# The preparation of a delta rule, carried along by the last tiles of an input projection

## The chip, the cores and the metric

The kernel runs on one core of a Trainium2 chip. The metric is the device time of one execution in microseconds. Each core has TensorE (PE in the profile; PEld is its weight loads), VectorE (DVE), ScalarE (ACT), GpSimd (POOL) and SyncE (SP, which here only issues transfers).

## The reference

One layer of a decoder, for 1024 prompt positions and 8 x 8 sample positions, so 1088 token columns in all. The normalised input is multiplied by w_in (1024 x 6400), whose first 1408 columns belong to branch A, the rest to branches B, C and three gates. Branch A, after a token shift, is RWKV-7 time mixing with six heads of 64:

```
w_log = -softplus(-(w0 + tanh(lw) @ w2)) - 0.5;  decay = exp(-exp(w_log))
a = sigmoid(a0 + la @ a2);  g = sigmoid(lg) @ g2
kk = k * k_k / max(sqrt(sum((k * k_k)^2)), 1e-12)        # per head
k = k * (1 + (a - 1) * k_a)
S = S * w_t + (S @ -kk_t) x (kk_t * a_t) + v_t x k_t;  out_t = S @ r_t
o = (groupnorm(out) * ln_w + ln_b + sum(r * k * r_k) * v) * g    # the bonus is the sum times v
```

Branches B and C are attentions; then the branches are merged by their gates, and an FFN follows.

## The kernel before

Everything is fp32 with tokens along the free dimension (T = 1088 columns) and features on the 128 partitions. `build` runs the stages in order, each a block of five instruction streams that wait for each other by semaphores, with a barrier between blocks: `stage_load` (loads and transposes x and the small weights), `a_project`, `a_prepare`, `a_delta_rule`, `a_finish`, then branch B, branch C, the merge and the FFN.

`a_project` goes over 50 tiles t of 128 columns of w_in. For each, SP loads 512 KB of weights into the one buffer `wt`, VectorE casts the high part into `wh` (L124), GpSimd subtracts for the low part `wl` (L129), and TensorE makes 3 chunks x 8 k-tiles x 3 products (L135 to L137) into PSUM banks 0 to 2 or 3 to 5 in turn. VectorE then scales the result into `raw` (L489). In VectorE's loop `weights(t + 1)` stands ahead of the eviction of tile t. Tiles 0 to 10 are branch A's: VectorE mixes in the token shift (L472 to L477) and keeps them in `pa`. Tiles 11 to 49 are stored to DRAM by ScalarE's queue (L455); from tile 26 on (the gates) ScalarE applies a sigmoid first (L453).

`a_prepare` makes from `pa` what the delta rule needs, for three pairs of heads (128 partitions each): two LoRA products (L543) and their sigmoids (L580); the squares of the keys, their sums per head (L548: nine matmuls of two columns), square root and reciprocal, spread again over the partitions (L565); a scan of the log decay (L634) and its exponentials (L596 to L598); the bonus (L559, L617); and the multiplications that leave r, k, a and kk scaled (L663 to L667). It holds `ld`, `cu`, `kk` for all three pairs and uses PSUM banks 0 to 6. The delta rule then works on `pa`, `g.av` and `g.at`; `a_finish` normalises its result, adds the bonus `g.bn` (L1285) and gates it.

Of the kernel before, what the change touches and what calls it, by code (L numbers as in the profile page):

```python
# [157 lines left out]
def build(nc, a, outs, scratch):  # L158

    with ExitStack() as ctx:  # L160
# [40 lines left out]
def stage_load(g):  # L201
# [8 lines left out]
    with ExitStack() as ctx:  # L210
# [3 lines left out]
        crow = sb("crow", [2 * NB, 2 * FF])  # L214
# [168 lines left out]
def stage_branch_a(g):  # L383

    nc = g.nc
    with ExitStack() as ctx:
        sb = lambda name, shape, dt=F32: ctx.enter_context(nc.sbuf_tensor(name, shape, dt))
        g.av = sb("av", [P, PAIRS, T])
        g.at = sb("at", [P, PAIRS, T])
        g.bn = sb("bn", [P, PAIRS, T])  # L390
        g.sc = sb("sc", [P, NU - 1, PAIRS])
        g.scs = sb("scs", [P, PAIRS, NB])
        a_prepare(g)
        a_delta_rule(g)
        a_finish(g)


def a_project(g):
# [3 lines left out]
    nc, a = g.nc, g.a  # L402
    w = a["w_in"][0].rearrange("(k p) f -> p k f", p=P)
    with ExitStack() as ctx:
# [4 lines left out]
        dif = sb("ap_dif", [P, 2, T])  # L409
        names = ("w", "wh", "ws", "mm", "ev", "z", "d", "mix", "sg")  # L410
# [4 lines left out]
        stores = lambda t: len(range(AT + (t - AT) % 2, t + 1, 2))  # L415
        with nc.Block() as block:
            @block.sync
            def _(eng):
# [4 lines left out]
                for i, sem in enumerate(g.s_xs):  # L423
                    eng.wait_ge(sem, 16 * len(range(i, SEQ // P + 1, len(g.s_xs))))
                eng.wait_ge(g.s_ls, 32)
                for t in (IN_TILES - 2, IN_TILES - 1):
                    eng.wait_ge(s_st[t % 2], 16 * stores(t))

# [7 lines left out]
            def _(eng):  # L436
                for t in range(IN_TILES):
# [18 lines left out]

            @block.vector
            def _(eng):
                nc.vector.memset(raw[:, :, 0:1], 0.0).then_inc(s["z"], 1)
                eng.wait_ge(s["z"], 1)  # L460

                def weights(t):
                    if t < IN_TILES:
                        eng.wait_ge(s["w"], 16 * (t + 1))
                        if t >= 2:
                            eng.wait_ge(s["mm"], t - 1)
                        high(eng, wh[:, t % 2], wt[:, :, :]).then_inc(s["wh"], 1)

                def mixed(t):
                    b = t % 2  # L470
                    eng.wait_ge(s["ev"], t + 1)
                    nc.vector.tensor_tensor(dif[:, b, :], raw[:, b, 0:T], raw[:, b, 1:1 + T], ALU.subtract).then_inc(s["d"], 1)  # L472
                    eng.wait_ge(s["d"], 2 * t + 1)
                    nc.vector.tensor_tensor(dif[:, b, SEQ:T:NQ], raw[:, b, 1 + T:1 + TP],
                                            raw[:, b, 1 + SEQ:1 + T:NQ], ALU.subtract).then_inc(s["d"], 1)
                    eng.wait_ge(s["d"], 2 * t + 2)
                    nc.vector.scalar_tensor_tensor(out=g.pa[:, t, :], in0=dif[:, b, :], scalar=g.col("rwkv_mu", t),  # L477
                                                   in1=raw[:, b, 1:1 + T], op0=ALU.mult, op1=ALU.add).then_inc(s["mix"], 1)

                weights(0)  # L480
                for t in range(IN_TILES):
                    weights(t + 1)
                    eng.wait_ge(s["mm"], t + 1)
                    if t >= 2:
                        eng.wait_ge(s["mix"], min(t - 1, AT))
                    if t >= AT + 2:
                        eng.wait_ge(s_st[t % 2], 16 * stores(t - 2))
                    for c, (c0, n) in enumerate(chunks(t)):
                        ins = nc.vector.tensor_tensor(raw[:, t % 2, 1 + c0:1 + c0 + n], g.ps[:, 3 * (t % 2) + c, 0:n],  # L489
                                                      g.inv[:, c0:c0 + n], ALU.mult)  # L490
                    ins.then_inc(s["ev"], 1)
                    if t < AT:
                        mixed(t)


def a_prepare(g):

    nc, a, pa, V_ = g.nc, g.a, g.pa, g.nc.vector  # L500
    R, K, V, LWA = 0, 3, 6, 9
    NJ = SEQ // P + 1
    rows = lambda j: P if j < NJ - 1 else TS
    RATE = -float(np.exp(-0.5))
    with ExitStack() as ctx:
        sb = lambda name, shape, dt=F32: ctx.enter_context(nc.sbuf_tensor(name, shape, dt))
        wa2 = sb("wa2", [P, AW])
        keep = sb("keep", [P, T])
        ld = sb("ld", [P, PAIRS, T])
        cu = sb("cu", [P, PAIRS, T])  # L510
        kk = sb("kk", [P, PAIRS, T])
        tmp = sb("tmp", [P, 2, T])
        ex = sb("ex", [P, 3, T])
        mid = sb("mid", [P, NU - 1, PAIRS])
        end = sb("end", [P, NU - 1, PAIRS])
        ends = sb("ends", [P, PAIRS, NB])
        omk = sb("omk", [P, PAIRS])
        nrm = sb("nrm", [P, PAIRS, NJ, 2])
        names = ("w", "th", "lo", "sg", "chain", "om", "kk", "tm", "cu", "ss", "rk", "bs", "bc", "took", "nm", "rt", "rv", "ex",
                 "ux", "end", "kn")  # L520
        s = {n: g.sem(f"pp_{n}") for n in names}
        cols = lambda t: t.rearrange("p (c n) -> p c n", n=CHUNK)
        turns = (("bs", 0), ("bs", 1), ("bc", 0), ("bs", 2), ("bc", 1), ("bc", 2))
        bank = lambda kind, p: 3 * (turns.index((kind, p)) % 2)
        sums = g.ps[:, 6, 0:PAIRS * NJ * 2].rearrange("t (p j h) -> t p j h", j=NJ, h=2)
        TILES = ((0, 512), (512, 512), (1024, TS))
        with nc.Block() as block:
            @block.sync
            def _(eng):
                eng.dma_start(wa2[0:HD, :], a["rwkv_w2"][0]).then_inc(s["w"], 16)  # L530
                eng.dma_start(wa2[HD:P, :], a["rwkv_a2"][0]).then_inc(s["w"], 16)

            @block.tensor
            def _(eng):
                eng.wait_ge(s["w"], 32)
                eng.wait_ge(s["th"], 1)
                for p in range(PAIRS):
                    for half in range(2):
                        if p:
                            eng.wait_ge(s["sg"], 2 * (p - 1) + half + 1)  # L540
                        at = slice(HD * half, HD * half + HD)
                        for c, (c0, n) in enumerate(CH):
                            mm = nc.tensor.matmul(g.ps[:, 3 * half + c, 0:n], wa2[at, p * P:(p + 1) * P],  # L543
                                                  pa[at, LWA, c0:c0 + n], start=True, stop=True)
                        mm.then_inc(s["lo"], 1)
                    eng.wait_ge(s["kk"], p + 1)
                    for j in range(NJ):
                        mm = nc.tensor.matmul(sums[0:rows(j), p, j], ex[:, p, j * P:j * P + rows(j)], g.blk[:, 0:P:HD],  # L548
                                              start=True, stop=True)
                    mm.then_inc(s["ss"], 1)  # L550
                eng.wait_ge(s["sg"], 2 * PAIRS)
                for q, (kind, p) in enumerate(turns):
                    if q >= 2:
                        eng.wait_ge(s["took"], q - 1)
                    b0 = bank(kind, p)
                    if kind == "bs":
                        eng.wait_ge(s["rk"], p + 1)
                        for c, (c0, n) in enumerate(CH):
# [12 lines left out]
            def _(eng):  # L571
# [4 lines left out]
                for p in range(PAIRS):  # L576
# [8 lines left out]
                    if p >= 2:  # L585
                        eng.wait_ge(s["rk"], p - 1)
# [2238 lines left out]
```

## Time and profile before

| | us |
|---|---|
| median of 3 runs | 2615.77 (2610.30 to 2619.48) |
| the profiled execution | 2620.84 |
| its span, first to last instruction | 2619.0 |
| TensorE busy | 2280.7 (87%) |
| VectorE, ScalarE, GpSimd busy | 1175.9, 426.3, 662.4 |
| mean granted TensorE clock | 0.925 |

The granted clock is given as a share of 2.4 GHz; it has two levels, 0.50 and 1.00, and a value between them is a mean. A busy TensorE is one that has a matmul in its pipeline.

### The profile page before, as it was taken

Reading aid. Unit: us, or ns where it says so; the run is one execution under the profiler, and the core shown is the slowest. Engines: PE = TensorE matmul, PEld = TensorE weight load, DVE = VectorE, ACT = ScalarE, POOL = GpSimd, SP = SyncE. Lnnn points to the kernel's source line nnn. Section 1 sums busy time; section 2 is a strip of 40 time slices with the busy share of each in tenths; the row PEclk is TensorE's granted clock in tenths of the full one; section 3 lists DMA queues with packets and bytes.
Section 4 is the critical chain, followed back from the end, with each engine's and each line's share of the span. In section 5 each row is a group of like instructions: output and inputs, shape, how many; then the busy total and the mean of one; then the engine's idle time right before and its main releaser. Section 6 shows DMA issues by size and latency. Waiting matters only on the chain. (4 is left out here: it accounts for less than half of the span.)

```text
span 2619.0 us, 45307 instructions
## 1 busy us (share of the span) xinstructions
PE 2280.7 (87%) x19175; PEld 2076.6 (79%) x19175; DVE 1175.9 (45%) x1702; ACT 426.3 (16%) x674; POOL 662.4 (25%) x607
## 2 busy tenths in 40 slices
PE   4999999999759986776777679799999999999985
PEld 3999999999548984434444556799999999999984
DVE  2341111111453323774764436138734743772752
ACT  4000001010411212661222401021000000100012
POOL 3212212121010000454440102333423422332331
PEclk6999999999779997897987789899999999999997
DMA  5112222222010001919996434311111111111112
GB/s 158 49 41 83 92 91 92 91 92 83 20 27 4 4 5 38 343 55 320 342 336 248 140 103 151 117 41 41 39 43 49 49 37 45 49 35 55 41 40 76
DMA packets 246309, 246.47 MB, mean 94 GB/s; under 512 B 23052, under 2 KB 225653, under 8 KB 244428
## 3 DMA queue, kind: packets, MB, share of 16 engines
q1 hardware_dynamic: 205248, 170.01, 20.9%
q10 hardware_dynamic: 32780, 51.50, 5.6%
q0 software_dynamic: 8080, 22.06, 2.5%
q8 instruction: 152, 2.49, 0.4%
q14 instruction: 49, 0.40, 0.0%
HBM read 206.89 MB, written 58.46 MB: 101 GB/s over the span
## 5 line engine op out<-in xcount | busy, mean ns | idle before, releaser
L135 PE MATMUL ps<-ml,fu_wh 128*128 128x352 f32 (+1 forms) x1248 | 409.8, 328 | 22.6 <-POOL fu_wl L129 17.5
L137 PE MATMUL ps<-mh,fu_wl 128*128 128x352 f32 (+1 forms) x1248 | 408.9, 328 | 0.0
L136 PE MATMUL ps<-mh,fu_wh 128*128 128x352 f32 (+1 forms) x1248 | 408.6, 327 | 0.0
L135 PE MATMUL ps<-xl_a,ap_wh 128*128 128x352 f32 (+2 forms) x1200 | 394.0, 328 | 8.8 <-POOL ap_wl L129 8.8
L136 PE MATMUL ps<-xh_a,ap_wh 128*128 128x352 f32 (+2 forms) x1200 | 394.8, 329 | 0.0
L137 PE MATMUL ps<-xh_a,ap_wl 128*128 128x352 f32 (+2 forms) x1200 | 393.9, 328 | 0.0
L489 DVE TENSOR_TENSOR ap_raw<-ps,inv 128x384 f32<-128x384 f32 x150 | 71.1, 530 | 463.9 <-PE ps L137 463.9
L135 PEld LDWEIGHTS ps<-ml,fu_wh 128*128 128x128 f32 x1248 | 235.7, 189 | 23.7 <-POOL fu_wl L129 23.7
L129 POOL TENSOR_TENSOR fu_wl<-fu_wt,fu_wh 128x1024 fp32r<-128x1024 f32 (+2 forms) x84 | 191.5, 2280 | 245.4 <-DVE fu_wh L124 245.4
L129 POOL TENSOR_TENSOR ap_wl<-ap_wt,ap_wh 128x1024 fp32r<-128x1024 f32 x50 | 120.2, 2404 | 478.4 <-DVE ap_wh L124 478.4
L136 PEld LDWEIGHTS ps<-mh,fu_wh 128*128 128x128 f32 x1248 | 236.4, 189 | 0.0
L137 PEld LDWEIGHTS ps<-mh,fu_wl 128*128 128x128 f32 x1248 | 235.3, 189 | 0.0
L135 PEld LDWEIGHTS ps<-xl_a,ap_wh 128*128 128x128 f32 x1200 | 226.0, 188 | 9.3 <-POOL ap_wl L129 9.3
L137 PEld LDWEIGHTS ps<-xh_a,ap_wl 128*128 128x128 f32 x1200 | 225.9, 188 | 0.0
L136 PEld LDWEIGHTS ps<-xh_a,ap_wh 128*128 128x128 f32 x1200 | 225.6, 188 | 0.0
L135 PE MATMUL ps<-fu_al,fu_wh 128*128 128x384 f32 x528 | 174.8, 331 | 10.8 <-POOL fu_wl L129 7.2
L137 PE MATMUL ps<-fu_ah,fu_wl 128*128 128x384 f32 x528 | 174.1, 330 | 0.0
L136 PE MATMUL ps<-fu_ah,fu_wh 128*128 128x384 f32 x528 | 173.3, 328 | 0.0
L2686 DVE TENSOR_TENSOR x<-x,ps 128x352 f32<-128x352 f32 (+1 forms) x120 | 56.6, 527 | 254.8 <-PE ps L137 254.8
L1608 PEld LDWEIGHTS ps<-cf,bs_pk 128*128 128x128 f32 x512 | 66.4, 161 | 74.3 <-DMA bs_pk<-in_cache_sb_k 56.0
L1608 PE MATMUL ps<-cf,bs_pk 128*128 128x128 f32 x512 | 82.0, 313 | 46.8 <-DMA bs_pk<-in_cache_sb_k 40.7
L2726 DVE TENSOR_TENSOR o<-ps,inv 128x384 f32<-128x384 f32 x132 | 59.5, 506 | 127.0 <-PE ps L137 127.0
(448 smaller groups left out, 3539.9 us busy)
## 6 DMA issues: line engine op xcount, KB each, us to landing
ap_wt<-in_w_in SPq DMA_DIRECT2D x50, 512.0 KB, 3.9
fu_wt<-in_w_up SPq DMA_DIRECT2D x44, 512.0 KB, 3.8
scr_pj<-ap_raw ACTq DMA_DIRECT2D x39, 544.0 KB, 2.7
out_win_sample<-in_cache_win SPq DMA_DIRECT2D x8, 2040.0 KB, 40.1
bs_pk<-in_cache_sb_k SPq DMA_DIRECT2D x112, 128.0 KB, 6.6
bs_pv<-in_cache_sb_v SPq DMA_DIRECT2D x112, 128.0 KB, 6.3
mg_gate<-scr_pj SPq DMA_DIRECT2D x24, 544.0 KB, 3.7
bs_pk<-in_cache_sb_k POOLq DMA_DIRECT2D x80, 128.0 KB, 5.7
```

What stands on the lines that cost most here:

```text
L129: return eng.tensor_tensor(dst.bitcast(F32R), x, xh, ALU.subtract)
L135: nc.tensor.matmul(out, wh, xl, start=start, stop=False)
L136: nc.tensor.matmul(out, wh, xh, start=False, stop=False)
L137: return nc.tensor.matmul(out, wl, xh, start=False, stop=stop)
L489: ins = nc.vector.tensor_tensor(raw[:, t % 2, 1 + c0:1 + c0 + n], g.ps[:, 3 * (t % 2) + c, 0:n], g.inv[:, c0:c0 + n], ALU.mult)
L1608: mm = nc.tensor.transpose(g.ps[:, 2 * (i % 2) + p, k * P:(k + 1) * P], pk[:, n % RK, i, k, p * P:(p + 1) * P], g.ident)
L2686: ins = V_.tensor_tensor(x1[:, t, c0:c0 + m], x1[:, t, c0:c0 + m], g.ps[:, 3 * (n % 2) + c, 0:m], ALU.add)
L2726: V_.tensor_tensor(u[:, h, 2 + c0:2 + c0 + m], g.ps[:, b0 + c, 0:m], inv[:, c0:c0 + m], ALU.mult)
```

## The change

`a_prepare` is gone. Its work for one pair of heads is cut into nine steps, k = 0 to 8, and `a_project` carries one step with each tile from t = 12 on: pair p's step k goes with tile 12 + 9p + k, so tiles 12 to 38. On TensorE the step's matmuls stand behind the tile's products, on ScalarE behind the tile's store, on VectorE behind the tile's eviction and ahead of the cast of the next weights. The steps use PSUM banks 6 and 7, which the products leave free, a bank of 512 columns at a time, and the six planes of `g.branches` as `ld`, `cu`, `kk`, `e0`, `e1` and `bn` for one pair at a time; `dif` lies there too. The scale exponentials come with tile 39. The bonus of a pair goes to DRAM by ScalarE's queue and is loaded back at the start of `a_finish`. `g.av`, `g.at` and the scales are allocated ahead of `stage_load`, whose state rows `crow` lie in them; SP loads the LoRA weights behind tile 2's weights; VectorE waits at the start of `a_project` until x and the shift rows are stored, for which SP waited at its end before.

What a pair's steps do on each engine (512, 512 and 64 are the columns of a bank's turn):

| k | TensorE | ScalarE | VectorE |
|---|---|---|---|
| 0 | LoRA w 512, 512 | 2 sigmoids | |
| 1 | LoRA w 64, LoRA a 512 | 2 sigmoids | memsets of e1 |
| 2 | LoRA a 512, 64 | 2 sigmoids, kk, square to e0 | scan, 3 small copies |
| 3 | 9 sums of squares | identity to e1 | max of sums, 2 subtractions |
| 4 | | square root | k times e1, r * k * r_k to at |
| 5 | bonus 512, 512 | exp to e0 | reciprocal, bonus 512, 512 |
| 6 | bonus 64, spread 512 | exp to e1 | bonus 64, kk 512, r times e0 |
| 7 | spread 512, 64 | store of the bonus, exp to e0 | kk 512, 64, k times e1, a times e1 |
| 8 | | | a times kk, at |

```diff
-                with tensor("pa", [P, AT, T]) as g.pa:
+                with tensor("pa", [P, AT, T]) as g.pa, tensor("avt", [P, 2 * PAIRS, T]) as g.avt, \
+                        tensor("sc", [P, NU - 1, PAIRS]) as g.sc, tensor("scs", [P, PAIRS, NB]) as g.scs:
+                    g.av, g.at = g.avt[:, 0:PAIRS, :], g.avt[:, PAIRS:2 * PAIRS, :]
+                    g.bonus = nc.dram_tensor("scr_bn", (PAIRS, P, T), F32, kind="Internal").ap()
...
-                        stage_branch_a(g)
+                        with ExitStack() as inner:
+                            delta(g, inner)
+                        a_finish(g)
...
-        crow = sb("crow", [2 * NB, 2 * FF])
+        crow = g.avt[0:2 * NB, :, :].rearrange("p k t -> p (k t)")[:, 0:2 * FF]
...
+        dif = g.branches[:, 0:2, :]
+        ld, cu, kk, e0, e1, bn = (g.branches[:, i, :] for i in range(6))
...
+        def step(t):
+            n = t - AT - 1
+            return divmod(n, STEPS) if 0 <= n < PAIRS * STEPS else (None, None)
+        LAST = AT + 1 + PAIRS * STEPS
...
-                for i, sem in enumerate(g.s_xs):
-                    eng.wait_ge(sem, 16 * len(range(i, SEQ // P + 1, len(g.s_xs))))
-                eng.wait_ge(g.s_ls, 32)
+                    if t == 2:
+                        eng.dma_start(wa2[0:HD, :], a["rwkv_w2"][0]).then_inc(s["wa"], 16)
+                        eng.dma_start(wa2[HD:P, :], a["rwkv_a2"][0]).then_inc(s["wa"], 16)
...
+                def lora(p, half, c, b):
+                    c0, n = TILES[c]
+                    at = slice(HD * half, HD * half + HD)
+                    nc.tensor.matmul(g.ps[:, 6 + b, 0:n], wa2[at, p * P:(p + 1) * P], pa[at, LWA, c0:c0 + n],
+                                     start=True, stop=True).then_inc(s["lo"], 1)
+                def bonus(p, c, b):
+                    c0, n = TILES[c]
+                    nc.tensor.matmul(g.ps[:, 6 + b, 0:n], g.blk, g.at[:, p, c0:c0 + n], start=True, stop=True).then_inc(s["bs"], 1)
+                def spread(p, c, b):
+                    for j in range(4 * c, min(4 * c + 4, NJ)):
+                        n = rows(j)
+                        for h in range(2):
+                            mm = nc.tensor.matmul(g.ps[HD * h:HD * h + HD, 6 + b, j % 4 * P:j % 4 * P + n],
+                                                  nrm[0:n, p, j, h:h + 1].broadcast_to([n, HD]), g.ident[0:n, 0:n],
+                                                  start=True, stop=True)
+                    mm.then_inc(s["bc"], 1)
+                def prepare(p, k):
+                    if k == 0:
+                        eng.wait_ge(s["wa"], 32)
+                        eng.wait_ge(s["th"], 1)
+                        eng.wait_ge(s["took"], 6 * p)
+                        lora(p, 0, 0, 0)
+                        lora(p, 0, 1, 1)
+                    elif k == 1:
+                        eng.wait_ge(s["lx"], 6 * p + 1)
+                        lora(p, 0, 2, 0)
+                        eng.wait_ge(s["lx"], 6 * p + 2)
+                        lora(p, 1, 0, 1)
+                    elif k == 2:
+                        eng.wait_ge(s["lx"], 6 * p + 3)
+                        lora(p, 1, 1, 0)
+                        eng.wait_ge(s["lx"], 6 * p + 4)
+                        lora(p, 1, 2, 1)
+                    elif k == 3:
+                        eng.wait_ge(s["lx"], 6 * p + 5)
+                        eng.wait_ge(s["kk"], p + 1)
+                        for j in range(NJ):
+                            mm = nc.tensor.matmul(g.ps[0:rows(j), 6, 2 * j:2 * j + 2], e0[:, j * P:j * P + rows(j)], g.blk[:, 0:P:HD],
+                                                  start=True, stop=True)
+                        mm.then_inc(s["ss"], 1)
+                    elif k == 5:
+                        eng.wait_ge(s["rk"], p + 1)
+                        eng.wait_ge(s["nm"], p + 1)
+                        bonus(p, 0, 0)
+                        eng.wait_ge(s["lx"], 6 * p + 6)
+                        bonus(p, 1, 1)
+                    elif k == 6:
+                        eng.wait_ge(s["took"], 6 * p + 1)
+                        bonus(p, 2, 0)
+                        eng.wait_ge(s["took"], 6 * p + 2)
+                        eng.wait_ge(s["rv"], p + 1)
+                        spread(p, 0, 1)
+                    elif k == 7:
+                        eng.wait_ge(s["took"], 6 * p + 3)
+                        spread(p, 1, 0)
+                        eng.wait_ge(s["took"], 6 * p + 4)
+                        spread(p, 2, 1)
...
                     mm.then_inc(s["mm"], 1)
+                    prepare(*step(t))
...
+                def sigmoid(p, half, c, b):
+                    c0, n = TILES[c]
+                    dst, par = ((ld, "rwkv_w0"), (g.av[:, p, :], "rwkv_a0"))[half]
+                    eng.wait_ge(s["lo"], 6 * p + 3 * half + c + 1)
+                    nc.scalar.activation(dst[:, c0:c0 + n], g.ps[:, 6 + b, 0:n], ACT.Sigmoid, bias=g.col(par, p)).then_inc(s["lx"], 1)
...
+                    elif k == 2:
+                        sigmoid(p, 1, 1, 0)
+                        sigmoid(p, 1, 2, 1)
+                        if p:
+                            eng.wait_ge(s["ux"], p)
+                        nc.scalar.activation(kk, pa[:, K + p, :], ACT.Copy, scale=g.col("rwkv_k_k", p))
+                        nc.scalar.activation(e0, pa[:, K + p, :], ACT.Square, scale=g.col("rwkv_k_k", p)).then_inc(s["kk"], 1)
...
+                    elif k == 7:
+                        eng.wait_ge(s["took"], 6 * p + 3)
+                        eng.dma_start(g.bonus[p], bn).then_inc(s["bn"], 16)
+                        eng.wait_ge(s["r0"], p + 1)
+                        nc.scalar.activation(e0, ld, ACT.Exp, scale=RATE).then_inc(s["ex"], 1)
...
+                for i, sem in enumerate(g.s_xs):
+                    eng.wait_ge(sem, 16 * len(range(i, SEQ // P + 1, len(g.s_xs))))
+                eng.wait_ge(g.s_ls, 32)
...
+                    elif k == 7:
+                        unit_keys(p, 1, 0)
+                        unit_keys(p, 2, 1)
+                        eng.wait_ge(s["ex"], 3 * p + 2)
+                        V_.tensor_tensor(pa[:, K + p, :], pa[:, K + p, :], e1, ALU.mult)
+                        link(V_.tensor_tensor(g.av[:, p, :], g.av[:, p, :], e1, ALU.mult))
+                    elif k == 8:
+                        eng.wait_ge(s["took"], 6 * p + 6)
+                        V_.tensor_tensor(g.av[:, p, :], g.av[:, p, :], kk, ALU.mult)
+                        eng.wait_ge(s["ex"], 3 * p + 3)
+                        V_.scalar_tensor_tensor(out=g.at[:, p, :], in0=kk, scalar=-1.0, in1=e0,
+                                                op0=ALU.mult, op1=ALU.mult).then_inc(s["ux"], 1)
...
+                eng.dma_start(bn[:, :, :], g.bonus.rearrange("a p t -> p a t")).then_inc(s["bn"], 16)
...
+                    eng.wait_ge(s["bn"], 16)
                     link(V_.scalar_tensor_tensor(out=om[:, p, :], in0=om[:, p, :], scalar=g.col("rwkv_ln_w", p),
-                                                 in1=g.bn[:, p, :], op0=ALU.mult, op1=ALU.add))
+                                                 in1=bn[:, p, :], op0=ALU.mult, op1=ALU.add))
                     eng.wait_ge(s["ge"], p + 1)
```

The removed `a_prepare` is printed above with the kernel; ScalarE's and VectorE's steps not shown here have its lines, with the waits of the step before. `link` makes VectorE wait for its own instruction, as before.

## Rows read from the trace of the kernel before

**Rows 1.** Busy slices of the page, TensorE: tenths, 40 slices of 65.475 us.
```profile
PE   4999999999759986776777679799999999999985
```

**Rows 2.** By stage: length; PE, PEld, DVE, ACT, POOL busy (instructions); clock, DMA share, GB/s.
```profile
203.00:667.00 464.00, 464.00 (x2802) 464.00 (x2801) 80.36 (x157) 27.03 (x24) 91.46 (x38) 1.00 0.26 88
...
674.30:756.00 81.70, 41.98 (x217) 30.76 (x217) 52.52 (x67) 32.60 (x42) 0.02 (x1) 0.63 0.01 3
```

**Rows 3.** Timeline, edges of the preparation: start, length, instruction.
```profile
674.30 0.56 SPq L530 DMA_DIRECT2D wa<-in_rwkv_w  x1
...
755.95 0.34 SPq L750 DMA_DIRECT2D dp_msk<-c_mask  x1
...
761.49 0.22 DVE L1081 MEMSET dp_st<- 128x192 f32 x1 [5.81 <-POOL dp_rk L774]
```

**Rows 4.** Timeline of TensorE in a_finish.
```profile
1012.88 2.05 PE L1198 MATMUL ps<-aux,af_sq 128*128 128x2 f32 x18
1014.86 2.10 PE L1189 MATMUL ps<-pa,g 128*128 128x384 f32 x6
1016.79 4.34 PE L1198 MATMUL ps<-aux,af_sq 128*128 128x2 f32 x36
...
1026.29 6.54 PE L1212 MATMUL ps<-cf,af_nrm 128*64 128x128 f32 x108
```

**Rows 5.** Timeline of TensorE, first products behind fp32 transposes in the FFN.
```profile
2536.78 0.42 PE L135 MATMUL ps<-fu_al,fu_wh 128*128 128x384 f32 x1
2537.03 0.33 PE L136 MATMUL ps<-fu_ah,fu_wh 128*128 128x384 f32 x1
```

**Rows 6.** TensorE by stretches: length, busy, granted clock, DMA share, GB/s.
```profile
1010.50:1016.80 6.30, 6.30 (x34) 1.00 0.00 0
1016.80:1020.40 3.60, 3.60 (x34) 1.00 0.02 5
1020.50:1023.50 3.00, 3.00 (x8) 0.50 0.00 0
...
686.00:688.00 2.00, 2.00 (x8) 0.50 0.00 0
```

**Rows 7.** Timeline of VectorE in a branch A tile; GpSimd's split on the page.
```profile
190.35 1.43 DVE L489 TENSOR_TENSOR ap_raw<-ps,inv 128x384 f32<-128x384 f32 x3 [7.05 <-PE ps L137]
...
194.63 0.69 DVE L124 CAST ap_wh<-ap_wt 128x1024 fp32r<-128x1024 f32 x1
202.36 1.43 DVE L489 TENSOR_TENSOR ap_raw<-ps,inv 128x384 f32<-128x384 f32 x3 [7.05 <-PE ps L137]
...
L129 POOL TENSOR_TENSOR ap_wl<-ap_wt,ap_wh 128x1024 fp32r<-128x1024 f32 x50 | 120.2, 2404 | 478.4 <-DVE ap_wh L124 478.4
```

**Rows 8.** Groups by form, VectorE and ScalarE in the preparation: count, busy us, mean ns, idle before.
```profile
L634 DVE TENSOR_TENSOR_SCAN cu<-keep,ld 128x1088 f32<-128x1088 f32 x3 | 7.2, 2416 | 7.3 <-ACT ld L580 7.3
...
L623 DVE TENSOR_TENSOR kk<-kk,ps 128x512 f32<-128x512 f32 x6 | 3.9, 683 | 5.8 <-PE ps L565 5.8
...
L664 DVE TENSOR_TENSOR pa<-pa,ex 128x1088 f32<-128x1088 f32 x3 | 3.9, 1283 | 0.0
...
L590 ACT ACT_TABLE_LOAD x1 | 1.3, 1283 | 0.0
```

**Rows 9.** Timeline of VectorE, first cast of w_in.
```profile
65.50 0.69 DVE L124 CAST ap_wh<-ap_wt 128x1024 fp32r<-128x1024 f32 x1 [3.62 <-DMA ap_wt<-in_w_in]
```

**Rows 10.** Timeline of a_finish's load and bonus; DMA issues, 1000 to 1060: KB, us to landing.
```profile
1004.43 0.34 SPq L1183 DMA_DIRECT2D g<-in_rwkv_g  x1
...
1030.09 1.35 DVE L1285 SCALAR_TENSOR_TENSOR om<-om,par,bn 128x1088 f32<-128x1088 f32 x1
...
qb<-scr_pj SPq DMA_DIRECT2D x6, 544.0 KB, 5.7
```

**Rows 11.** Timeline of TensorE in the preparation, second pair's sums and third pair's LoRA.
```profile
689.07 3.88 PE L548 MATMUL ps<-aux,ex 128*128 128x2 f32 x18
692.88 5.44 PE L543 MATMUL ps<-pa,wa 64*128 64x384 f32 x12
```

More of the change, by code:

```diff
@@ L380, in _ @@
                     V_.tensor_copy(last[:, h * 512:(h + 1) * 512], g.ps[0:NB + 1, 6 + h, :]).then_inc(s["lc"], 1)
[L383 to L395, printed above, removed]
 def a_project(g):
-    nc, a = g.nc, g.a
+    nc, a, pa, V_ = g.nc, g.a, g.pa, g.nc.vector
     w = a["w_in"][0].rearrange("(k p) f -> p k f", p=P)
+    R, K, V, LWA = 0, 3, 6, 9
+    NJ = SEQ // P + 1
+    rows = lambda j: P if j < NJ - 1 else TS
+    RATE = -float(np.exp(-0.5))
+    TILES = ((0, 512), (512, 512), (1024, TS))
+    STEPS = 9
     with ExitStack() as ctx:
@@ L408, in a_project @@
         raw = sb("ap_raw", [P, 2, 1 + TP])
-        dif = sb("ap_dif", [P, 2, T])
-        names = ("w", "wh", "ws", "mm", "ev", "z", "d", "mix", "sg")
+        wa2 = sb("wa2", [P, AW])
+        mid = sb("mid", [P, NU - 1, PAIRS])
+        end, ends = g.sc, g.scs
+        omk = sb("omk", [P, PAIRS])
+        nrm = sb("nrm", [P, PAIRS, NJ, 2])
+        dif = g.branches[:, 0:2, :]
+        ld, cu, kk, e0, e1, bn = (g.branches[:, i, :] for i in range(6))
+        names = ("w", "wh", "ws", "mm", "ev", "z", "d", "mix", "sg", "wa", "th", "lo", "lx", "om", "kk", "ss", "nm", "rt", "rv", "tm",
+                 "cu", "rk", "bs", "bc", "took", "ex", "r0", "e1", "ux", "chain", "bn", "end", "scan")
         s = {n: g.sem(f"ap_{n}") for n in names}
@@ L455, in _ @@
                     eng.dma_start(g.pj[t - AT], row(t)).then_inc(s_st[t % 2], 16)
[L457 to L493, printed above, removed]
@@ new lines, in bonus, with unit_keys @@
+                def bonus(p, c, b):
+                    c0, n = TILES[c]
+                    eng.wait_ge(s["bs"], 3 * p + c + 1)
+                    V_.tensor_tensor(bn[:, c0:c0 + n], g.ps[:, 6 + b, 0:n], pa[:, V + p, c0:c0 + n], ALU.mult).then_inc(s["took"], 1)
+                def unit_keys(p, c, b):
+                    c0, n = TILES[c]
+                    eng.wait_ge(s["bc"], 3 * p + c + 1)
+                    V_.tensor_tensor(kk[:, c0:c0 + n], kk[:, c0:c0 + n], g.ps[:, 6 + b, 0:n], ALU.mult).then_inc(s["took"], 1)
@@ new lines, in _ @@
+                weights(0)
+                for t in range(IN_TILES):
+                    weights(t + 1)
+                    eng.wait_ge(s["mm"], t + 1)
+                    if t >= 2:
+                        eng.wait_ge(s["mix"], min(t - 1, AT))
+                    if t >= AT + 2:
+                        eng.wait_ge(s_st[t % 2], 16 * stores(t - 2))
+                    for c, (c0, n) in enumerate(chunks(t)):
+                        ins = V_.tensor_tensor(raw[:, t % 2, 1 + c0:1 + c0 + n], g.ps[:, 3 * (t % 2) + c, 0:n],
+                                               g.inv[:, c0:c0 + n], ALU.mult)
+                    ins.then_inc(s["ev"], 1)
+                    if t < AT:
+                        mixed(t)
+                    if t == AT:
+                        k0 = PROWS["rwkv_k_a"][0]
+                        V_.tensor_scalar(omk[:, :], g.par[:, k0:k0 + PAIRS], -1.0, 1.0, ALU.mult, ALU.add).then_inc(s["om"], 1)
+                        link(V_.memset(nrm[TS:P, :, NJ - 1, :], 1.0))
+                    prepare(*step(t))
+                    if t == LAST:
+                        link(V_.tensor_tensor(end[:, :, :], end[:, :, :], mid[:, :, :], ALU.subtract))
+                        V_.tensor_tensor(end[:, 0:NU - 2, :], end[:, 0:NU - 2, :], mid[:, 1:NU - 1, :], ALU.add).then_inc(s["end"], 1)
```

247 lines of the change are left out of this document (91 added, 156 removed).

## The prediction

> **What bounds the kernel now.** I read the busy slices first [rows 1]: TensorE is at 9 tenths from the second slice on, falls to 7 and 5 in the two slices from 654.75 to 785.7 us, and is full again after. The table by stage says what lies there [rows 2]: while w_in is multiplied (203 to 667 us) TensorE is busy 464.00 of 464.00 us at a granted clock of 1.00 (2.4 GHz), and VectorE only 80.36; in the preparation, 674.30 to 756.00, TensorE is busy 41.98 of 81.70 us at 0.63, VectorE 52.52, ScalarE 32.60, and no engine fills it: it is a dependency chain through three engines. So one stage is bound by TensorE with the other two engines mostly free, and the next is bound by waits. The edges come from the timeline [rows 3]: the preparation's first instruction is SP's load at 674.30, and the delta rule's first is SP's load at 755.95. The last products of w_in end a little after 667; the roughly 7 us from there to 674.30 (eviction, sigmoid, last store, the barrier) belong to w_in's end and stay.
>
> **What goes.** The whole of a_prepare as a stage: 755.95 - 674.30 = 81.65 us [rows 3]. After the change the delta rule begins where the preparation began. Nothing more is gained there, whatever clock TensorE starts it with: VectorE's first work in it, at 761.49, has waited 5.81 us for GpSimd to clear the masked tiles [rows 3], which starts only with the stage.
>
> **What is added on TensorE, which is full.** Per pair of heads: two LoRA products over 1088 columns, the nine 2-column sums of squares, one bonus product over 1088 columns, the spreading of the reciprocals. a_finish has the same shapes at a clock of 1.00, one behind the other, so the distance of the starts is the price [rows 4]: sums 1014.86 - 1012.88 = 1.98; 1088 columns 1016.79 - 1014.86 = 1.93 (the LoRA has 64 rows instead of 128; I take the same, since columns set it); spreading 6.54 / 3 = 2.18. One pair costs 2 x 1.93 + 1.98 + 1.93 + 2.18 = 9.95, three pairs 29.85 us. All of it delays the next tile, since TensorE has no gap to put it into.
>
> **Stepping in and out.** Seven of nine steps have TensorE work (all but 4 and 8), so 21 times the stream of products is broken. Where the FFN's end puts fp32 transposes between products, the first product afterwards stands 2537.03 - 2536.78 = 0.25 us ahead of the next [rows 5], against 464.00 / 2802 = 0.166 in the stream [rows 2]: 0.08 lost per step, 1.7 us in all. From below it is nothing; from above I take the whole 0.25, 5.3 us. I take 1.7, as the row has the same two kinds of work meeting.
> The Trainium skill (TensorE: Matmul & The Clock Gate, Single matmul latency) gives a lone matmul a fixed part of about 166 ns at the full clock that a stream hides; exposed at both edges of 21 steps that would be an estimate of 7.0 us in place of 1.7, and the saving 5.3 us less. The row above shows half of one such part, so it speaks against the page's full price.
>
> **The clock.** The 2-column sums keep TensorE occupied but hardly stream. With one pair's sums between long products the clock stayed at 1.00 (1010.50 to 1016.80); with two pairs' in a row, 1016.80 to 1020.40, it fell right after, and 1020.50 to 1023.50 ran at 0.50, the 1.2 GHz level; and in the preparation, after the first pair's sums, 686 to 688 ran at 0.50 [rows 6]. So one pair's sums held once and fell once. In the change there are three, each inside full products. A fall lasted somewhat over 3 us and half of that is lost, say 1.7. None: 0; all three: 5.1; I take one, 1.7.
>
> **VectorE's steps, costed at nothing.** They stand between a tile's eviction and the cast of the next weights (L124), on which GpSimd's subtraction (2.40 us) and then TensorE wait. Tiles of branch A already have such work there: eviction starts at 190.35, the cast only at 194.63, and still VectorE then stands 7.05 us until the products end at 202.36 [rows 7]. The cast could come 202.36 - 194.63 - 0.69 - 2.40 = 4.6 us later before TensorE notices. That is 2.85 us of work after the 1.43 us eviction, plus 4.6: a step may last 7.4 us. The longest is step 7, two multiplications from PSUM (at most 0.68 each) and two of 1.28: 3.9 us; step 2 has the scan, 2.42, and three small copies; step 3 waits for the sums (1.98 against 1.43, so 0.6) and has two full-width ops, about 3.5 [rows 8]. Cover left: 3.5 us. If it were gone, each us over it would cost a us per tile. The single weight buffer's load starts later too, by the same 3.9 at most; it lands during the tile, whose length is 11.92 us (72 x 0.166).
>
> **ScalarE's steps, costed at nothing.** All of them are 32.60 us [rows 2], 1.2 us a tile over 27 tiles. Where gate tiles (from 26) meet Exp or Sqrt steps, the table changes twice in a tile, 1.28 us each [rows 8]: with the row's sigmoid and a step's work it stays near 6 us of 11.92. Its row store is behind nothing but its own sigmoid; behind the step's waits stand only the next tile's sigmoid and store, and the raw buffer that they free is wanted two tiles later.
>
> **Queues and waits.** SP issues two small loads after tile 2's weights, ahead of tile 3's, which waits for a split anyway. ScalarE's queue carries three more stores of 544 KB, reused nine tiles later. VectorE's new wait at the start (x and the shift rows stored) stands ahead of the first cast, which has waited 3.62 us, until 65.50, for its weights [rows 9]; the shift stores, 36 KB against 512, are issued on the same queue ahead of that load: 0, at worst a microsecond. The bonus comes back in one load of three 544 KB planes behind g2, issued about 1004.8; VectorE reads it from 1030.09; the six 544 KB loads of the next stage take 5.7 us each, all together [rows 10]. Cover 25 us against about 6: nothing.
>
> **Sum.** -81.65 + 29.85 + 1.7 + 1.7 = -48.4. The profiled execution took 2620.84 us (span 2619.0 and 1.84 around it), so 2572.4; the median of the three runs, 2615.77, is 5.07 lower, so 2567.4 on the scale of the runs.
>
> **Rivals.**
> *The clock falls and stays down (0.12).* For it: in the preparation the same LoRA products ran at 0.50 for most of their time although TensorE counted as busy [rows 2, 11]. Against it: there they stood among stands and sums, here each step of at most 2 us lies in 11.92 us of full products that hold 1.00. At half speed a pair costs 5.44 (LoRA) + 3.88 (sums) [rows 11] + 2 x 1.93 + 2 x 2.18 = 17.5, three 52.6; with 5.3 for stepping the saving is 81.65 - 57.9 = 23.8: 2592.0. If only a third of the steps drag a fall of 1.7 behind them (7 x 1.7 = 11.9 in place of 1.7), it is 2577.6.
> The Trainium skill (the same page, LDWEIGHTS) makes the weight load's time depend on columns alone, not on the clock; then the sums, which are nearly all weight loads, would stay at 1.98 and this rival be 5.7 us cheaper. The rows disagree: 3.88 at 0.50 against 1.98 at 1.00, so it keeps its price.
> *The bonus is late (0.03).* If the load took 35 us instead of 6, a_finish would stand 10 us: 2577.4. Six loads of this size at the next stage's start speak against it.
> *TensorE stands at the steps' semaphores: slower (0.02).* Each step waits for VectorE or ScalarE, and in the old preparation exactly such waits made the idle time. If a step needed a result of its own tile it would wait out an eviction and an operation; from 48.4 / 21 = 2.3 us per step on the change gains nothing, and at 4 us it loses 36: 2651. Against it: I followed every wait in TensorE's steps, and each names work released one tile earlier, which has 11.92 us for at most 6.
> *It doesn't overlap after all (0.03).* A wait that I misread holds some steps up to the break-even: within 8 us of before. That the preparation ends late is excluded: its last step is at tile 38 and the scale exponentials at 39 of 50, over 100 us before the end.
>
> **How the numbers follow.** The likeliest (0.80) has the sum's own bounds: no stepping cost and no fall, 2564.0; all 5.3 and 5.1, 2574.4. The runs of before lie from 5.5 below to 3.7 above their median, and 0.3% (7.8 us) is about what this kernel's measurement can tell from no change; so 2558 to 2578 for it, which also holds the milder half of the first rival and the late bonus. To leave out no more than 2 in 10 I set the range at 2556 to 2581. Faster by over 0.3%: 0.80 + 0.12 + 0.03 = 0.95; same 0.03; slower 0.02.
>
> **What would show it.** Right: nothing between w_in's end and the delta rule but the same 7 us or so; tiles 12 to 38 of w_in some 33 us longer in all, with TensorE still full, 1.3 to 2.3 us more where a step has its work and none at steps 4 and 8; clock 1.00 except perhaps after step 3; VectorE at about 53 us more in w_in's stage; delta rule and a_finish as long as before. Wrong: TensorE idle ahead of its step's first matmul (a semaphore), ahead of L135's first product (weights late), a clock of 0.50 over whole tiles, or VectorE standing for the bonus load in a_finish.

## The result, and the profile after

The changed kernel takes 2570.70 us (median of 4 runs, 2568.07 to 2572.30) against 2614.41 for the kernel before (4 runs, 2610.30 to 2619.48): a ratio of 0.9829, 95% interval 0.9807 to 0.9850. The forecast was 2567.4 in a range of 2556 to 2581.

The slices of the page, now 64.2 us each, answer to [rows 1]: the dip of 7 and 5 is gone and the delta rule follows the full slices. The table by stage answers to [rows 2]: TensorE busy 500.00 of 500.00 us at clock 1.00, with VectorE 54.3 and ScalarE 60.0 us up on 36 us more of stage.
```profile
PE   3999999999989976857777687999999999999985
```
```profile
203.00:703.00 500.00, 500.00 (x3019) 485.18 (x3017) 134.66 (x236) 87.01 (x88) 91.25 (x38) 1.00 0.25 85
```
The edges, from the timeline, answer to [rows 3]: the last eviction of w_in, and 6.68 us later the delta rule's first load, whose VectorE still waits for GpSimd. Then the bonus in the finish, answering to [rows 10].
```profile
703.27 1.42 DVE L691 TENSOR_TENSOR ap_raw<-ps,inv 128x384 f32<-128x384 f32 x3 [10.51 <-PE ps L137]
...
709.95 0.34 SPq L779 DMA_DIRECT2D dp_msk<-c_mask  x1
...
715.49 0.22 DVE L1110 MEMSET dp_st<- 128x192 f32 x1 [10.80 <-POOL dp_rk L803]
...
958.71 0.43 SPq L1214 DMA_DIRECT2D af_bn<-scr_bn  x1
...
985.54 1.35 DVE L1317 SCALAR_TENSOR_TENSOR om<-om,par,af_bn 128x1088 f32<-128x1088 f32 x1
```
The price of each step is read from the starts of two evictions. From tile 11 on, the starts for tiles without a step are 11.93 us apart in both kernels; here 266.49 - 253.15 = 13.34, so step 2 costs 1.41:
```profile
253.15 1.42 DVE L691 TENSOR_TENSOR ap_raw<-ps,inv 128x384 f32<-128x384 f32 x3 [9.73 <-PE ps L137]
254.48 2.42 DVE L639 TENSOR_TENSOR_SCAN o<-o 128x1088 f32<-128x1088 f32 x1
...
257.31 0.69 DVE L124 CAST ap_wh<-ap_wt 128x1024 fp32r<-128x1024 f32 x1
...
266.49 1.42 DVE L691 TENSOR_TENSOR ap_raw<-ps,inv 128x384 f32<-128x384 f32 x3 [8.48 <-PE ps L137]
```
Worked out so, the us added by each step of the first pair (the other pairs agree within 0.03 except where noted; "stage" is from the first eviction to the last, 585.46 before). The rows e1 to e12 are the experiments below, one trace each; e10 and e11 leave the steps alone, and their stage is the changed kernel's within 0.02:

| kernel | 0 | 1 | 2 | 3 | 4 | 5 | 6 | 7 | 8 | stage |
|---|---|---|---|---|---|---|---|---|---|---|
| changed | 2.11 | 1.26 | 1.41 | 2.09 (3rd pair 3.64) | 0 | 1.71 | 1.39 | 1.48 | 0 | 621.28 |
| e1 full height | 1.72 | 1.08 | 1.08 | 2.08 (2nd, 3rd 3.63) | 0 | 1.72 | 1.38 | 1.49 | 0 | 620.10 |
| e8 first LoRA full | 1.71 | 1.42 | 1.42 | 2.08 (3rd 3.62) | 0 | 1.72 | 1.39 | 1.48 | 0 | 620.56 |
| e9 second LoRA full | 2.11 | 1.41 | 1.08 | 3.63 (3rd 2.08) | 0 | 1.72 | 1.39 | 1.48 | 0 | 622.28 |
| e12 halves in turn | 1.25 | 1.26 | 0.56 | 2.09 (3rd 3.62) | 0 | 1.71 | 1.39 | 1.48 | 0 | 616.14 |
| e2 wide spread | 2.11 | 1.26 | 1.41 | 2.09 (3rd 3.64) | 0 | 1.71 | 1.12 | 1.45 | 0 | 620.39 |
| e3 sums split | 2.11 | 1.26 | 1.41 | 1.13 | 0.96 | 1.72 | 1.39 | 1.48 | 0 | 619.75 |
| e4 sums twice | 2.11 | 1.26 | 1.41 | 7.24, 5.70, 7.27 | 0 | 1.72 | 1.39 | 1.48 | 0 | 633.67 |
| e5 more VectorE | 2.11 (2nd, 3rd 2.87) | 1.26 | 1.41 | 3.62 (2nd, 3rd 2.09) | 0 | 1.72 | 1.39 | 1.48 | 0.37 | 628.30 |
| e6 sums early | 2.11 | 1.25 | 11.69, 11.37, 11.81 | 0 | 0 | 1.72 | 1.38 | 1.49 | 0 | 644.11 |
| e7 three together | 1.71 | 1.09 | 1.07 | 1.13 | 0.97 | 1.71 | 1.12 | 1.45 | 0 | 616.14 |

In the changed kernel a pair costs 11.4 us, three 34.3, and one fall of the granted clock 1.55: 621.28 - 585.46 = 35.8, forecast 33.25.

The two profiled spans differ by 2619.0 - 2569.0 = 50.0 us: -81.65 for the preparation, +35.8 for the tiles, and -4.2 elsewhere: the finish +1.43 (958.31 to 997.56, 39.25 in place of 37.82), all that follows it -5.36, and -0.28 ahead of it. The medians differ by only 43.7, and -81.65 + 35.8 + 1.4 is -44.4, so the -5.36 is hardly the change's: the profiled execution of before (2620.84) lay 6.4 above its median. In the 14 traces of the study the stages behind the finish take 1567.4 to 1576.8, before's the longest; the finish takes 37.7 to 39.4 in the traces that leave it alone, so whether its 1.4 is the change's isn't shown. The experiments below are therefore read by the table and not by their single total times.

### The profile page after: what moved, and what is told of

It is laid out like the page before. It is cut to its first block and busy times, and to the rows that moved or that the text cites. A ratio compares the mean times of both kernels' runs of the same rounds, so it can differ in the third digit from the quotient of the medians.

```text
span 2569.0 us, 45346 instructions
## 1 busy us (share of the span) xinstructions
PE 2267.7 (88%) x19175; PEld 2062.1 (80%) x19175; DVE 1178.1 (46%) x1714; ACT 452.4 (18%) x695; POOL 663.2 (26%) x607
## 5 line engine op out<-in xcount | busy, mean ns | idle before, releaser
L1640 PE MATMUL ps<-cf,bs_pk 128*128 128x128 f32 x512 | 78.7, 304 | 50.0 <-DMA bs_pk<-in_cache_sb_k 43.7
```

The source lines that it names most:

```text
L1640: mm = nc.tensor.transpose(g.ps[:, 2 * (i % 2) + p, k * P:(k + 1) * P], pk[:, n % RK, i, k, p * P:(p + 1) * P], g.ident)
```

## Experiments

In the code, `...` stands for what is left out.

**Why the steps cost more than their columns (e1, e8, e9, e12).** By the bonus step, 1024 columns cost 1.71 us, so 576 would cost 0.96. Steps 0 to 2, with 1024, 576 and 576 columns, cost 2.11, 1.26 and 1.41. The weight loads and products of the changed kernel, at step 0 (64-row LoRA) and at step 5 (128-row bonus):
```profile
225.81 0.29 PEld L454 LDWEIGHTS ps<-pa,wa 64*128 64x128 f32 x2 [0.23 <-issue]
226.35 0.19 PEld L454 LDWEIGHTS ps<-pa,wa 64*128 64x128 f32 x1 [0.24 <-issue]
226.78 0.19 PEld L454 LDWEIGHTS ps<-pa,wa 64*128 64x128 f32 x1 [0.24 <-issue]
227.72 0.19 PEld L135 LDWEIGHTS ps<-xl_a,ap_wh 128*128 128x128 f32 x1 [0.76 <-issue]
...
292.08 0.35 PEld L459 LDWEIGHTS ps<-avt,aux 128*128 128x128 f32 x2
...
293.53 0.19 PEld L135 LDWEIGHTS ps<-xl_a,ap_wh 128*128 128x128 f32 x1 [0.24 <-issue]
```
```profile
225.56 0.32 PE L137 MATMUL ps<-xh_a,ap_wl 128*128 128x352 f32 x1
225.81 1.98 PE L454 MATMUL ps<-pa,wa 64*128 64x512 f32 x4
227.72 0.44 PE L135 MATMUL ps<-xl_a,ap_wh 128*128 128x384 f32 x1
228.00 0.34 PE L136 MATMUL ps<-xh_a,ap_wh 128*128 128x384 f32 x1
...
292.24 1.88 PE L459 MATMUL ps<-avt,aux 128*128 128x512 f32 x4
293.55 0.74 PE L135 MATMUL ps<-xl_a,ap_wh 128*128 128x384 f32 x1
```
Into the LoRA the first weights load after a gap of 0.23, and out of it the next main weights load only when the LoRA is over (227.72, gap 0.76); at the bonus both lie inside the stream (no gap at 292.08; 293.53, while the bonus runs). Each product is two passes over its columns (x4 for two products), and inside the LoRA the passes follow each other at 0.43 us (226.35 and 226.78 are where the second and third begin), which is 1.67 ns for each column of a product. From the last main product (225.56) to the LoRA's second pass it is 0.79 where 0.16 + 0.43 would do, and from there to the second main product (228.00) 1.65 where 3 x 0.43 + 0.17 would: some 0.2 is lost on the way in and 0.2 on the way out. Is it the height?

e1 gives both LoRAs 128 rows, with zeros in the other half's weights:
```
-  nc.tensor.matmul(..., wa2[at, p * P:(p + 1) * P], pa[at, LWA, c0:c0 + n], ...)
+  nc.tensor.matmul(..., wa2[:, p, half, :], pa[:, LWA, c0:c0 + n], ...)
```


> The LoRA matmuls read their whole 128 rows: the weights of the two LoRAs lie in a zeroed 128-row block, so that each reads all of the LoRA input and its other half counts for nothing. Columns, waits and results stay as they are. In the changed kernel the steps 0, 1 and 2 lengthen a tile by 2.10, 1.26 and 1.41 us for 1024, 576 and 576 columns, while the bonus step 5 with 1024 columns of 128 rows lengthens it by 1.71. Theory A, hand-over: the half-high matmuls hold back the load of the next weights, and full-height ones don't. Then step 0 falls to about 1.71, steps 1 and 2 to about 1.0 each, some 1.0 us for each pair and 3 us in all. Theory B, stepping: what a step costs above its columns is its waits and semaphores, which stay. Then the steps keep 2.10, 1.26 and 1.41 and the sum doesn't move.

Measured: 1.72, 1.08, 1.08, or 0.90 us less per pair, 2.7 in all, with TensorE's waits unchanged. So it is the height, and theory B falls. The stage is only 1.18 shorter since two pairs had a clock fall here instead of one (2567.62 us in all). At full height the LoRA's weights load in the stream like the bonus's:
```profile
224.15 0.35 PEld L455 LDWEIGHTS ps<-pa,avt 128*128 128x128 f32 x2
...
225.60 0.19 PEld L135 LDWEIGHTS ps<-xl_a,ap_wh 128*128 128x128 f32 x1 [0.24 <-issue]
```
e8 and e9 make one LoRA full and leave the other half high:
```
+  at = slice(0, P) if half == 0 else slice(HD * half, HD * half + HD)    # e8; half == 1: e9
```


> Only the first LoRA's matmuls read 128 rows (the second LoRA's stay half high, on rows 64 to 127). Full height took 0.38, 0.18 and 0.34 us from steps 0, 1 and 2. Step 0 has two products of the first LoRA, step 1 one of 64 columns of the first and then one of 512 of the second, step 2 two of the second. Exit theory: what counts is that the last product ahead of the main ones is half high, so that the next main weights can't be loaded behind it. Then step 0 takes 1.72, step 1 stays at 1.26 and step 2 at 1.41. Entry theory: it is the first load of a step that is held; then step 0 takes 1.72, step 1 falls to 1.08 and step 2 stays at 1.41. If both ends cost, step 1 lies halfway, about 1.17.

> The other way round: only the second LoRA's matmuls read 128 rows. Exit theory: step 0 stays at 2.10, step 1 (whose last product is now full) falls to 1.08, step 2 to 1.08. Entry theory: 2.10, 1.26 and 1.08. Both ends: step 1 about 1.17.

Measured: with one full and one half-high product step 1 takes 1.42 in e8 and 1.41 in e9, whichever comes last, and more than with both half high (1.26). All three values that were expected are missed: it is 0.45 above its 576 columns either way, as step 2 with its two half-high products. (2569.08 and 2567.75 us.) That agrees with the trace of step 0 above: either order goes into half height once and out of it once, whichever product comes last. What is left odd is the 1.26: one product of 64 columns on rows 0 to 63 and one of 512 on rows 64 to 127.

e12 puts such a pair into every step (the waits of ScalarE and VectorE follow the new order):
```
   k == 0:  lora(p, 0, 0, 0)
-           lora(p, 0, 1, 1)
+           lora(p, 1, 0, 1)
   k == 1 and 2 likewise: tile 1 of both, then tile 2 of both
```


> The LoRA products stay half high, but each step takes one of the first LoRA (rows 0 to 63) and one of the second (rows 64 to 127) of the same columns: 1024, 1024 and 128 columns in steps 0, 1 and 2, in place of 1024, 576 and 576. The two runs before it showed that half-high products cost 0.33 to 0.38 us in a step with one of them or with two of the same half, and 0.18 in the only step with one of each half. Theory, two different halves next to each other cost half: steps 0 and 1 take 1.71 + 0.18 = 1.9 each (step 0 was 2.10), some 0.2 us less where 1024 columns are concerned. Rival, a step's visit to half-high products costs 0.33 to 0.38 whatever they are, and the 0.18 came from its 64 columns: steps 0 and 1 take 2.05 to 2.10 each. In step 2, 128 columns, 0.5 to 0.6 by either. VectorE's scan waits for ScalarE of its own tile here, about 1 us, within the limit.

Measured: 1.25, 1.26, 0.56; both expectations fall, the result is far better. Step 0's 1024 columns cost 0.85, the price of 512, and 0.40 above. The two products, on different halves of the rows, run side by side. The trace shows it: the weights of all four passes load within 0.30 us, where the changed kernel's third and fourth came at 226.35 and 226.78, a pass apart, and the four passes take 1.13 us, where one behind the other they would take at least 4 x 0.43:
```profile
224.44 0.32 PE L137 MATMUL ps<-xh_a,ap_wl 128*128 128x352 f32 x1
224.70 1.13 PE L454 MATMUL ps<-pa,wa 64*128 64x512 f32 x4
225.76 0.44 PE L135 MATMUL ps<-xl_a,ap_wh 128*128 128x384 f32 x1
```
```profile
224.70 0.30 PEld L454 LDWEIGHTS ps<-pa,wa 64*128 64x128 f32 x4 [0.23 <-issue]
```
With that all the half-high LoRA steps fit one sum, made after the runs: columns at 1.67 ns, counted once where two halves run together, and 0.39 to 0.45 for a visit to half height, in and out: 1.71 + 0.40, 0.85 + 0.41, 0.96 + 0.45, and e12's 0.11 + 0.45. The LoRA of a pair falls from 4.78 to 3.07 us, the stage by 5.1; one run took 2564.52 us.

**The spreading (e2).** VectorE writes the reciprocals out over 128 columns, and TensorE needs 9 matmuls for 18:
```
-  for h in range(2): matmul(ps[HD * h:HD * h + HD, ...], nrm[0:n, p, j, h:h + 1].broadcast_to([n, HD]), ...)
+  matmul(ps[:, ...], wide(p, j)[0:n, :], g.ident[0:n, 0:n], ...)
```


> The reciprocals are spread over 128 columns by VectorE first (two copies more in its step 5), so that TensorE spreads each block of 128 tokens with one matmul of 128 weight columns in place of two of 64: 9 in place of 18 for each pair. The LoRA weights only lie elsewhere. Steps 6 and 7 lengthen a tile by 1.38 and 1.48 us in the changed kernel. By columns alone the nine matmuls of 1088 columns and the bonus tile's 64 columns would still take about 1.95 us, for 128 weight columns are loaded for each either way. Theory A, hand-over at matmuls that use part of the array: steps 6 and 7 fall to about 1.0 each, some 0.9 us for each pair, 2.6 in all. Theory B, stepping by waits: they stay at 1.38 and 1.48. If VectorE's longer step 5 (some 1.3 us more on 3 to 4) reached TensorE, step 6 would grow instead.

Measured: 1.12 and 1.45; 0.3 us per pair, a third of what theory A expected (2568.96 us). Going from one product to the next is not what these steps mainly pay for: nine matmuls cost about as much as 18 half as wide. The expectation took 1.95 for these columns; what the rest of the 2.57 is stays open.

**The clock (e3, e4).** In the changed kernel the third pair's sums are followed by half-clock products; the timeline, and the table by stretches (TensorE's clock after the five engines' busy times):
```profile
503.95 2.05 PE L491 MATMUL ps<-aux,o 128*128 128x2 f32 x18
505.92 0.44 PE L135 MATMUL ps<-xl_a,ap_wh 128*128 128x384 f32 x1
...
507.57 0.52 PE L135 MATMUL ps<-xl_a,ap_wh 128*128 128x384 f32 x1
```
```profile
507.50:508.50 1.00, 1.00 (x4) 1.00 (x4) 1.00 (x1) 0.99 (x1) 0.00 (x0) 0.50 0.96 392
509.90:511.00 1.10, 1.10 (x8) 1.10 (x7) 0.00 (x0) 0.00 (x0) 1.10 (x1) 1.00 0.00 0
```
e3 does five of the nine sums in step 3 and four in step 4; e4 does all nine twice in step 3.
```
e3:  k == 3: for j in range(5): ...      k == 4: for j in range(5, NJ): ...
e4:  k == 3: for j in 2 * tuple(range(NJ)): ...
```


> Of the nine two-column sums of a pair five are done at step 3 and four at step 4, and VectorE's maximum waits until step 4. Clock theory: the third pair's step 3 takes 3.63 us in place of 2.08 because the granted clock falls to 0.50 behind the sums' two microseconds without wide matmuls; a stretch half as long doesn't bring it down. Then steps 3 and 4 together take 2.1 to 2.4 us in all three pairs, and the stage gets about 1.5 us shorter. Rival: the fall has to do with the place in time and not with the sums' length; then one of the three still shows about 3.6, or another tile does.

> The nine two-column sums of a pair are done twice in step 3 (the second time over the first, same values), so that the stretch without wide matmuls is about 4 us and not 2. Clock theory: the granted clock falls to 0.50 in all three pairs, each fall costs about 1.55 us, and step 3 takes about 5.6 us in each: some 9 us more in all. Rival, a fall by chance once in three: steps 3 take 4.1, 4.1 and 5.6, some 6 us more in all. A third way: the fall begins inside the longer sums and they themselves run at half speed, up to 2 us more for each pair, 11 to 15 us in all.

Measured: e3's steps 3 and 4 take 1.13 + 0.96 = 2.09 in every pair, with no fall, 1.5 us less in the stage (2571.28 us in all, given back by other stages). e4's step 3 takes 5.70 once and 7.24 and 7.27 twice: the clock falls in all three, in two of them already within the sums, as the third way had it; +12.4 in the stage, 2584.26 us. In the first pair the 36 passes take 5.04 us, and the granted clock is 0.50 by their end:
```profile
264.44 5.04 PE L491 MATMUL ps<-aux,o 128*128 128x2 f32 x36
269.41 0.69 PE L135 MATMUL ps<-xl_a,ap_wh 128*128 128x384 f32 x1
```
```profile
266.00:267.00 1.00, 1.00 (x11) 1.00 0.12 48
267.00:268.00 1.00, 1.00 (x9) 0.67 1.01 405
268.00:269.00 1.00, 1.00 (x6) 0.50 0.34 121
```
So the fall follows the sums: 18 in a row brought it in three pairs of three, in two of them before the sums were over, which e3's rival, the place in time, doesn't explain. Over all nine kernels of the study with nine sums in step 3, 11 of 27 pairs had a fall, each of 1.53 to 1.55 us; with five and four (e3, e7), none of 6, which by the odds of 11 in 27, pair by pair, would come about once in 23 times. Which of the pairs it takes isn't fixed by the program: it is the third in the changed kernel, e10 and e11, the first in e5, which up to there does the same work.

**VectorE's limit (e5).** Two more multiplies in step 4, six more in step 8, all unused.
```
+  for _ in range(2): link(V_.tensor_tensor(e1, pa[:, V + p, :], pa[:, V + p, :], ALU.mult))   # step 4
+  for _ in range(6): link(V_.tensor_tensor(cu, pa[:, V + p, :], pa[:, V + p, :], ALU.mult))   # step 8
```


> VectorE does work that nothing uses: two multiplies over 1088 elements more (about 1.28 us each) at step 4, six more at step 8. The prediction costs VectorE's steps at nothing as long as they end within 7.4 us of the tile's eviction. Step 4 becomes about 5.2 us of VectorE: the theory expects its tile unchanged. Step 8 becomes about 10.3 us: the next tile's first mixes come about 2.9 us too late, and TensorE stands that long at the new tile's inputs, some 8.7 us in all for three pairs. Rival, VectorE's limit is nearer than worked out: step 4 already lengthens its tile by up to 2.6 us, and the sum is 12 to 16. Rival, VectorE has no limit here (tiles buffered further): nothing moves.

Measured: step 4 unchanged. After step 8 TensorE stands for GpSimd's split of the weights, 1.06 us where the next pair's LoRA comes first and needs no new weights, and 2.97 where no step follows, the 2.9 of the theory:
```profile
345.07 1.98 PE L454 MATMUL ps<-pa,wa 64*128 64x512 f32 x4
348.11 0.44 PE L135 MATMUL ps<-xl_a,ap_wh 128*128 128x384 f32 x1 [1.06 <-POOL ap_wl L129]
...
588.01 0.45 PE L135 MATMUL ps<-xl_a,ap_wh 128*128 128x384 f32 x1 [2.97 <-POOL ap_wl L129]
```
The stage grew by 7.0 instead of 8.7: the LoRA covers most of two of the three stands, and behind the third the clock fell too (the next evictions are 16.35 apart, 4.4 over 11.93). In all 2571.45 us; other stages gave the difference back in that one execution, those behind the finish 4.0 of it.

**A stand at a semaphore (e6).** TensorE's sums move to the step in which ScalarE makes what they read.
```
   k == 2:  lora(p, 1, 2, 1)
-  k == 3:
            wait lx 6p + 5;  wait kk p + 1;  sums
```


> TensorE's nine sums move from step 3 into the end of step 2, the step in which ScalarE makes the squares that they read; the work is the same. This is the rival of the prediction in which TensorE stands at a step's semaphore. Theory: ScalarE's two sigmoids, the copy and the square (about 4 us) come after the LoRA products, so TensorE waits about 3 to 4 us in step 2; step 2 takes 6.5 to 7.5 us and step 3 about 0, some 3 to 4 us for each pair, 9 to 12 us in all. After the wait the granted clock may fall too, 1.5 to 2.5 us more where it does. Rival, the semaphore comes in time: step 2 takes 1.41 + 2.08, step 3 nothing, the sum 0.

Measured: step 2 takes 11.4 to 11.8, step 3 nothing, 2591.57 us. TensorE stands 3.86 us, as expected, but the stand costs twice that: the clock falls during it and is at 0.50 when the sums begin, they take 3.85 in place of 2.05, and the products after them run at half speed too. 11.69 - 1.41 - 2.09 = 8.2 us for a stand of 3.9.
```profile
258.31 3.85 PE L490 MATMUL ps<-aux,o 128*128 128x2 f32 x18 [3.86 <-ACT o L546]
262.10 0.69 PE L135 MATMUL ps<-xl_a,ap_wh 128*128 128x384 f32 x1
262.58 0.52 PE L136 MATMUL ps<-xh_a,ap_wh 128*128 128x384 f32 x1
```
**The bonus (e10, e11).** The load repeated, two and five times one behind the other.
```
+  for i in range(2):      # e11: range(5)
+      if i: eng.wait_ge(s["bn"], 16 * i)
       eng.dma_start(bn[:, :, :], g.bonus.rearrange("a p t -> p a t")).then_inc(s["bn"], 16)
```


> The finish of branch A loads the bonus twice, one load behind the other, and waits for the second. One load took 7.2 us from issue to landing, was issued at 958.7, and its first reader started at 985.5: 26.8 us of cover. Theory (the load is costed at nothing as long as it lands in that cover): two loads land some 15 us after the first issue, and the finish keeps its 39.2 us, or 37.8 where its clock falls later. Rival, the load takes something from the stage beside it although it lands in time: 1 to 7 us more.

> The same with five loads in a row. At 7.2 us each they land 36 us after the first issue, and some 0.3 us more for each hand-over, 9 to 11 us after the first reader could have started: the finish grows by 9 to 11 us and its VectorE stands at the first sum with the bonus for a DMA. Rival: the loads take less when nothing runs beside them, 5.7 us as other loads of this kernel do; then they are 2 to 4 us late.

Measured: with two the finish takes 39.30 (2570.89 us), nothing more. With five, four of them at 6.4 to 6.5 us and one at 8.0, VectorE stands 7.22 and the finish takes 46.42, 7.2 more, between the two expectations (2579.79 us):
```profile
994.73 1.35 DVE L1320 SCALAR_TENSOR_TENSOR om<-om,par,af_bn 128x1088 f32<-128x1088 f32 x1 [7.22 <-DMA af_bn<-scr_bn]
```
**Together (e7).** The edits of e1, e2 and e3 in one kernel.

> Full-height LoRA matmuls, reciprocals spread by VectorE with nine matmuls in place of 18, and the sums split five and four over steps 3 and 4, together. If the hand-over theory and the clock theory both hold, the stage loses 3.0 + 2.6 + 1.5, about 7 us: 2564 us beside 2570.7, and beside the kernel before a ratio of 0.980 to 0.981. If what a step costs is its waits, it is 0 to 1.5 us, which can't be told from the changed kernel by total time; then the tiles' periods decide.

Measured in five runs: 2565.87 us (2562.91 to 2567.62) against 2614.74, ratio 0.9815, interval 0.9800 to 0.9829. The stage is 5.1 shorter instead of 7: 2.7 from e1, 1.6 from e3 and no fall in any pair, but 0.9 from e2 where 2.6 was expected. All its runs lie below all four of the changed kernel's, by 0.45 us at the nearest. e12's order in place of e1's padding, with e2 and e3, would give another 2.4 by the table; that is an estimate and wasn't run.

## Why the prediction was right, step by step

- **What goes:** the preparation's 81.65 us went whole; hand-over (6.54 and 6.68) and delta rule (248.48 and 248.36) kept their lengths.
- **What is added on TensorE, and stepping:** the forecast was 9.95 of work and 7 x 0.08 of stepping for a pair, 10.5; measured 11.4. By term: LoRA 4.78 for 3.86, sums 2.09 for 1.98, bonus and spreading together 4.58 for 4.11. This is the mis-sized part: above the work stand 4.4 us for three pairs in place of the 1.7 in "Stepping in and out", 2.7 short. The row it rested on [rows 5] was of full-height work. "I take the same, since columns set it" failed for the LoRA: with 64 rows a visit costs some 0.4 us, and step 1 saved columns by running two halves side by side. At the bonus step even 0.08 was too much: its 1.71 is its four passes at 0.43. Why the spreading took more than in a_finish stays open. The Trainium skill's fixed part (TensorE: Matmul & The Clock Gate, Single matmul latency), from which the prediction made an estimate of 7.0 us, was too high on the sum: this trace has 4.4, and nothing at the bonus step.
- **The clock:** one fall of three was taken, 1.7; there was one, 1.55. That it hangs on the sums' length is shown by e4, and e3 and e7 agree. That it was just one is partly chance: seven of the nine kernels with these sums had one, two had two. By the Trainium skill (TensorE: Matmul & The Clock Gate, LDWEIGHTS) the sums' time doesn't hang on the clock; e6 disagrees, as [rows 11] did: 3.85 at 0.50, 2.05 at 1.00.
- **VectorE, ScalarE, queues at nothing:** TensorE had no gap in the stage; 7.4 us as VectorE's limit is borne out by e5, the bonus's cover by e10 and e11. ScalarE's own sum was too low: 60.0 us came to the stage in place of 32.60, mostly since its table is loaded 23 times in place of 3, at 1.28 us each; the prediction named these changes and left them out of the sum. ScalarE had the time, so this cost nothing.
- **The rivals:** clock staying down, bonus late, no overlap: none showed. The stand at a semaphore didn't occur, but was priced too low: 4 us of it cost 8 (e6), so by that price some six stands, and not all 21 steps at 2.3, would have eaten the gain.
- **The scale:** by the medians the change saves 43.7 where 48.4 was forecast, 4.7 less: 2.6 in the tiles, 1.4 in the finish if its one trace of before is typical, and 0.7 that no row assigns. The forecast time is only 3.3 off, since the kernel before came out at 2614.41 in place of 2615.77. The sum for the profiled execution, 2572.4, is 1.8 off, and that it is so near is luck: 2.6 too little for the tiles met 4.2 that the other stages gave.

## What to carry to other kernels

Here a stage that was bound by waits could be laid into one that is bound by TensorE nearly for the price of its matmuls, because each TensorE step reads only what was made a tile earlier; a stand of 3.9 us there cost its length again in clock, while stands of 1.06 brought no fall (e5). Price the matmuls by height: products on the two halves of the rows belong next to each other, where they ran at once, and products of 64 rows that have no partner were cheaper padded to 128. Keep stretches of narrow sums short, here five in place of nine.

## What the hardware showed that was not expected

Two 64-row fp32 matmuls of 512 columns on different row halves took 1.13 us in the trace, where two on the same half took 1.98. A step with half-high products between full ones cost 0.39 to 0.45 us above its columns, at step 0 half on the way in and half on the way out; one of 128 rows cost nothing above them at 1024 columns and 0.12 at 576. Nine fp32 sums of two columns, 2 us in which TensorE counts as busy, were followed by a fall of the granted clock to 0.50 in 11 of 27 pairs, and 18 in a row brought it down in 3 of 3. A stand of 3.9 us brought it to 0.50 and cost 8.2.
